# Moving the top-k pieces of two token tiles between pairs of gathered expert rows

## The reference

```python
v1, i1 = lax.top_k(s1, PEER_TOPK)
v2, i2 = lax.top_k(s2, PEER_TOPK)
cand = v1[..., :, None] + v2[..., None, :]          # 16 x 16 sums
top_s, top_c = lax.top_k(cand, PEER_TOPK)
...
act = gelu(einsum('ckd,cd->ck', expert_u[idx], x))
out = einsum('ck,ckd->cd', softmax(top_s) * act, expert_v[idx])
```

## Time and profile before

| | us |
|---|---|
| median of 3 runs | 3334.22 (3332.88 to 3334.69) |
| profiled execution | 3336.84 |
| its span | 3334.7 |
| TensorE, VectorE busy | 2621.3, 2133.8 |
| ScalarE, GpSimd busy | 1085.6, 1192.0 |
| first gather issued | 297.2 |
| moved by DMA | 1272.02 MB |

### The profile page before, as it was taken

One profiled execution on the slowest core, in us unless ns is written; L12 is line 12 of the kernel. 1 busy time (PEld: TensorE's weight loads), 2 busy tenths in 40 slices (PEclk: granted clock), 3 DMA queues, 4 the chain that ended last, 5 costly groups with the idle time before them and its releaser, 6 DMA issues.

```text
span 3334.7 us, 40436 instructions
## 1 busy us (share of the span) xinstructions
PE 2621.3 (79%) x14560; PEld 1321.0 (40%) x14560; DVE 2133.8 (64%) x4998; ACT 1085.6 (33%) x3411; POOL 1192.0 (36%) x1048
## 2 busy tenths in 40 slices
PE   8998878998888788998878777998885555555565
PEld 6775534564454344553444333554351111111111
DVE  2324669776568887775458878675448656765444
ACT  2112344332332643322323553332322232222222
POOL 0001333333334443333333443333334444444443
PEclk9999999999999899999899989999888777777777
DMA  4356999999999999999999989999999999999998
GB/s 135 112 158 242 416 385 343 399 392 402 404 416 417 409 398 417 418 417 415 415 417 408 396 349 413 418 418 416 412 415 405 412 420 421 419 417 412 420 421 337
DMA packets 224534, 1272.02 MB, mean 381 GB/s; under 512 B 24912, under 2 KB 26960, under 8 KB 93264
## 3 DMA queue, kind: packets, MB, share of 16 engines
q0 software_dynamic: 147456, 1073.81, 78.5%
q1 hardware_dynamic: 64128, 161.56, 13.2%
q10 hardware_dynamic: 12752, 34.08, 2.6%
HBM read 1256.78 MB, written 12.58 MB: 381 GB/s over the span
## 4 chain that ended last, share of the span: by engine, by line
DMA 39%; PE 34%; DVE 12%; issue 6%; ACT 5%; POOL 3%; ACTq 0%; POOLq 0%; DVEq 0%; SPq 0%
DMA rowsb<-uv,e_idx 38%; PE yacc L886 14%; PE mixp L583 7%; DVE rowsb L1678 5%; POOL rowsb L955 3%; PE mixp L608 3%; PE mixp L634 2%; PE mixp L595 2%; ACT diag L1241 2%; DVE area L1331 2%; ACT wg L1236 2%; PE mixp L645 2%; PE yacc L583 1%; DMA wt<-w_query_ 1%; ACT gmt L1222 1%
## 5 line engine op out<-in xcount | busy, mean ns | idle before, releaser
L955 POOL DMA_INDIRECT rowsb<-uv,e_idx x1024 | 1187.8, 1160 | 2114.9 <-PE yacc L886 1659.7
L1678 DVE CUSTOM_DVE_ANT_0 rowsb<-rowsb,hnrow 128x1024 f32<-128x1024 f32 x1024 | 1241.2, 1223 | 826.3 <-DMA rowsb<-uv,e_idx 824.5
L886 PE MATMUL yacc<-rowsb,diag 64*64 64x512 f32 x8192 | 1223.7, 722 | 660.7 <-ACT diag L1241 651.7
L886 PEld LDWEIGHTS yacc<-rowsb,diag 64*64 64x64 f32 x8192 | 300.0, 151 | 1406.7 <-ACT diag L1241 981.6
L1222 ACT ACTIVATE gmt<-dots 128x2 f32<-128x2 f32 x512 | 104.1, 203 | 1714.3 <-DVE dots L1678 1713.8
L583 PE MATMUL mixp<-area,wt 128*128 128x256 f32 x2144 | 497.7, 386 | 1.2 <-ACT area L1019 1.2
L583 PEld LDWEIGHTS mixp<-area,wt 128*128 128x128 f32 x2144 | 400.5, 191 | 128.3 <-issue 78.1
L1241 ACT ACTIVATE diag<-ident,wg 128x64 f32<-128x64 f32 x1024 | 300.3, 340 | 16.7
L1236 ACT ACTIVATE wg<-gmt,gate 128x1 f32<-128x1 f32 x1024 | 245.6, 286 | 17.7
L973 ACT ACTIVATE area<-mixp 128x512 f32<-128x512 f32 (+3 forms) x334 | 148.0, 487 | 290.6 <-PE mixp L583 167.7
L608 PE MATMUL mixp<-area,wt 128*128 128x256 f32 x960 | 229.2, 393 | 6.7 <-DMA wt<-w_query_ 6.7
(11 more groups left out here) (213 smaller groups left out, 1770.7 us busy)
## 6 DMA issues: line engine op xcount, KB each, us to landing
wt<-w_merge SPq DMA_DIRECT2D x96, 512.0 KB, 8.0
wt<-w_feat SPq DMA_DIRECT2D x80, 512.0 KB, 7.9
wt<-w_query_ SPq DMA_DIRECT2D x64, 512.0 KB, 12.1
wt<-w_tok SPq DMA_DIRECT2D x32, 512.0 KB, 10.7
wt<-w_out_ SPq DMA_DIRECT2D x32, 512.0 KB, 7.9
rowsb<-uv,e_idx POOLq DMA_INDIRECT x1024, 13.6
area<-x_rows ACTq DMA_DIRECT2D x4, 1024.0 KB, 12.4
area<-keysT ACTq DMA_DIRECT2D x16, 256.0 KB, 11.6
```

The costliest lines, as they stand in the source:

```text
L886: last = pe.matmul(yacc[at:at + HP, k % 2, c * NCH:(c + 1) * NCH], diag[r * HP:(r + 1) * HP, s, :], rowsb[r * HP:(r + 1) * HP, s, D + c * ...
L955: pool.indirect_dma_start(rowsb[:, n % RS, :], None, uv, bass.IndirectOffsetOnAxis(ap=e_idx[:, i % 2, k:k + 1], axis=0)).then_inc(row_load ...
L1678: dve.tensor_tensor_reduce(rowsb[:, s, 0:D], rowsb[:, s, 0:D], hnrow[:, i % HR, :], 1.0, 0.0, ALU.mult, ALU.add, dots[:, s:s + 1]).then_in ...
```

## The change

The table of the first 63 pieces becomes one piece in each of the pairs 2 to 37 and 57 to 83, numbered through the tiles, and none in 38 to 56. Before, there was one in each of 2 to 19, then 9 over pairs 20 to 39, then 36 over 40 to 82. The third group of the first tile's pieces listed here (heads 6 and 7) so ends at pair 28 in place of 39, and the second tile's four groups at 37, 65, 74 and 83 in place of 50, 61, 72 and 82. The load of the last scores and the softmax entries are moved with them, and the first tile's norm, final norm and store come three pairs later. The planner reads the table, so the steps of the second block may be laid otherwise.

```diff
--- before.py
+++ after.py
@@ -391,9 +391,9 @@
         cost = [load_of(b) for b in range(NB)]
         del cost[0][N_NORM + N_PROJ1:N_NORM + N_PROJ1 + n_sba(0)]
         TOP_EACH, BLOCK_END = 9, 36
-        SCORES_AT = (12, 13, 21, 41)
-        GATES = ((1, 0, 1, 1), (11, 0, 2, 2), (20, 0, 4, 2), (40, 0, 6, 2),
-                 (62, 1, 0, 2), (65, 1, 2, 2), (74, 1, 4, 2), (84, 1, 6, 2))
+        SCORES_AT = (12, 13, 21, 30)
+        GATES = ((1, 0, 1, 1), (11, 0, 2, 2), (20, 0, 4, 2), (30, 0, 6, 2),
+                 (62, 1, 0, 2), (67, 1, 2, 2), (76, 1, 4, 2), (85, 1, 6, 2))
         GATES_AT = {slot: n for n, (slot, i, first, count) in enumerate(GATES)}
         N_SLOT = TT * PP
         N_PARTS = 4 * TOP_EACH
@@ -407,14 +407,8 @@
                 else:
                     due = (p - 15) * N_PARTS // 42
                 parts_at[i][p] = max(0, min(due, N_PARTS)) - sum(parts_at[i][:p])
-        for n in range(83):
-            i, p = divmod(n, PP)
-            if n < 20:
-                parts_at[i][p] = 1 if n >= 2 else 0
-            elif n < 40:
-                parts_at[i][p] = (n - 19) * TOP_EACH // 20 - (n - 20) * TOP_EACH // 20
-            else:
-                parts_at[i][p] = (n - 39) * N_PARTS // 43 - (n - 40) * N_PARTS // 43
+        for n in [*range(2, 38), *range(57, 84)]:
+            parts_at[n // PP][n % PP] = 1
 
 
         def slot_load(s):
@@ -1261,11 +1255,11 @@
                     for p in range(PP):
                         gelu(i, p)
                         spread(i, p)
-                        if i == 1 and p == 19:
+                        if i == 1 and p == 22:
                             act.wait_ge(experts_ready, 8)
-                        if i > 0 and p == (19 if i == 1 else 3):
+                        if i > 0 and p == (22 if i == 1 else 3):
                             norm(i - 1)
-                        if i > 0 and p == (23 if i == 1 else 7):
+                        if i > 0 and p == (26 if i == 1 else 7):
                             store_out(i - 1)
                         if p == (36 if i == 1 else 20):
                             load_h(i)
@@ -1720,7 +1714,7 @@
                             next(parts, None)
                         if i * PP + p - 1 in GATES_AT:
                             gates(*GATES[GATES_AT[i * PP + p - 1]][1:])
-                        if i > 0 and p == (21 if i == 1 else 5):
+                        if i > 0 and p == (24 if i == 1 else 5):
                             final_norm(i - 1)
                         for b in range(NB):
                             for _n in range(steps[i * PP + p][b]):
```

## The result

The changed kernel takes 3347.18 us (median of 6 runs, 3342.95 to 3352.26) against 3333.55 (median of 6, 3330.93 to 3334.76) for the kernel before: a ratio of 1.0044, 95% interval 1.0033 to 1.0055, that is 11 to 18 us slower. The forecast was 3342.2, range 3331 to 3349. Its profiled execution took 3345.53 us with a span of 3343.3.

What follows compares the result with a forecast made beforehand. The expert stage was taken to be bound by bytes, VectorE and TensorE starving the transfers in places. Terms 7.8 + 0 + 3 + 0 - 2.8 = +8.0 us on the median 3334.22 gave 3342.2 us, range 3331 to 3349.

Steps and rivals of the forecast that it cites:

- What bounds the kernel: Expert stage, about 297 us to the end: bound by bytes; reordering can win only 35.6 us of transfers below their rate.
- Part 1: Pairs 24 to 37: added pieces less moved steps and a shorter wait make +5.3 us, 7.8 us more lost in transfers.
- Part 2: Quiet pairs 38 to 56: TensorE is full, so removing VectorE's pieces there gives nothing back, 0 us.
- Part 3: Pairs 57 to 83, 27 pieces for 22: crowding in pairs 62 to 66 costs 3 us, bounds 0 and 5.5.
- Part 4: Moved gate exponentials, score load, norm and store: nothing waits for them, 0 us.
- Part 5: Pairs 62 to 66: eight row buffers hide part of TensorE's lateness, 2.8 us off, bounds 0 and 6.
- C: Pairs 38 to 61: VectorE's pieces starve transfers, so the quiet pairs pay; -7 us, 3327; chance 0.15.
- B: Buffers hide the second half: part 3 nothing, part 5 its full size; +2 to +5 us, 3337; chance 0.25.
- D: Whole kernel: the change does not bind, planner's shift and pieces cancel; 3334; chance 0.10.

Runs made afterwards that it cites:

- e10_front_only: The kernel before with its steps and dates, but one piece in each of pairs 2 to 37 and the last 27 evenly over 38 to 82: ratio 1.0037.
- e2_pieces_only: The changed kernel with pieces and all dates as in the change, but the second block's steps laid as before: 3351.58 us, ratio 1.0057.
- e6_back_only: The kernel before, with 10 pieces evenly in pairs 38 to 56, 27 in 57 to 83 and the late dates, steps unmoved: ratio 1.0008.
- e1_shift_only: The kernel before with its pieces and dates, only the second block's steps laid as the changed planner lays them: 3337.38 us, ratio 1.0010.
- e4_dates_only: The kernel before with pieces and steps unmoved, only the second tile's gates and first tile's norm and store late: 3333.91 us, ratio 1.0006.

## Why the prediction was right, and where it was off

The forecast had the direction and most of the mechanism, but not the split, and that the measured time lies inside the range is partly luck. In the unit of its own sum, transfers below their rate: part 1 was 7.8 and measured 4.8, part 2 was 0 and measured 0.8 + 4.0, parts 3 and 5 together were 0.2 and measured 4.0, and 0.3 came behind. A first term too large by 3.0 covered a third of what the others lacked.

**What bounds the kernel**: right. The time is that of the transfers, and the sum of their losses gives the difference of the medians (14.0 against 13.6).

**Part 1, pairs 24 to 37**: the stretch was to take 96.1 + 5.3 and took 101.3 us, where the working gives 101.4. Pair 38 itself came at 573.8 for 575.7, since pair 24 started 1.7 us earlier. The price of a piece read from pairs with and without one held, with unmoved steps too: 12.7 us for 12.5 worked out (`e10_front_only`). Where the softmax and the score load moved to pair 30 with the pieces it was 19.3 (`e2_pieces_only`). Its loss in transfers came out smaller, 4.8 for 7.8, because 325 GB/s were still moved. (The heading's "eight more" is a slip, the text's 8 and 18 are right; it enters no sum.)

**Part 2, the quiet pairs**: that they give nothing back was right. VectorE has 72.85 us of work in place of 94.81 between these sums, and the stretch is still 138.4 us long, where 136.6 were worked out; with 12 or 17 pieces in it it is no longer (136.8, 137.9). The Trainium skill, Perfetto Trace Analysis, section Identifying the Most-Contended Engine, holds matmul busy time to be no good measure and judges TensorE's headroom by the weight-load share among others. Here that share was 56%, and it was no room: this case goes with the busy time. The size was off. In transfers, 0 was forecast and 4.8 us were lost more, with 385 GB/s in place of 398: filling pair 52 was counted as 1.9 us less of TensorE and not as transfers that find less time. The sum of pair 42 came at 604.15 for 602.4, that of pair 62 at 742.51 for 739.0, so +9.95 for +6.4. Part of it is in pairs 38 to 42: 26.5 us, where 6.2 and three times 5.60 were taken. These rows of the changed kernel's TensorE show it:

```profile
569.65 3.69 PE L880 MATMUL yacc<-rowsb,diag 64*64 64x512 f32 x16 [5.56 <-ACT diag L1235]
573.27 4.72 PE L577 MATMUL mixp<-area,wt 128*128 128x256 f32 x16
577.92 0.60 PE L732 MATMUL mixp<-ident,area 4*128 4x4 f32 x4
578.45 1.95 PE L880 MATMUL yacc<-rowsb,diag 64*64 64x512 f32 x16
580.33 3.72 PE L577 MATMUL mixp<-area,wt 128*128 128x256 f32 x16
585.77 1.95 PE L880 MATMUL yacc<-rowsb,diag 64*64 64x512 f32 x16 [1.73 <-ACT diag L1235]
```

It had stood still for 5.56 us while VectorE was behind; the sum and the weight unit that follow take 3.69 and 4.72 us for 1.95 and 3.72, VectorE waits 2.36 us for the small matmul behind them (L732), and then each waits for the other once more (1.73). Two engines that each need 5.6 and 5.5 us a pair took 6.6 here, not the larger of the two.

**Part 3, the crowd**: mechanism and place were right (pair 64, the residual, TensorE's wait for it), the size was not: from the sum of pair 62 to that of pair 66 (774.69) it took 32.2 us, before 24.8 (757.34), +7.4 for the 3 that I took and the 5.5 of the upper bound. (By the prices of part 1 the five pieces are 10.1 us and not 10.3.) I had the normalizer's steps beside the residual in the text, but counted only the pieces; the reciprocal in the same pair and the lower clock of TensorE's sum and unit were left out. Between the same two sums the crowd alone adds 3.4 us (28.2, `e6_back_only` and `e2_pieces_only`) and the shift alone 1.8 (26.6, `e1_shift_only`). So the 3 fits the crowd by itself; the shift's 1.8 and 2.2 more where the two meet were not counted.

**Part 4, dates**: the late ones are right, 0 (`e4_dates_only`, 1.0006, interval across 1, at most 5 us). For the softmax at pair 30, 0 fits the change, where VectorE has no wait for it, but the reason given is not enough. That its scores are ready does not make it free: it puts two table loads of 1.28 us in front of a gelu, and with unmoved steps pair 38 came 6.6 us later for it. That the planner had emptied just pair 30 was luck. No run moves this date alone.

**Part 5, what the buffers hide**: right in kind, too small. At TensorE's sums the forecast was 6.4 + 1.25 (the weight unit not yet fetched) + 3 - 2.8 = 7.9; measured it is 9.95 + 1.25 + 7.4 = 18.6 by pair 66, of which 13.6 arrived, so 5.0 were hidden. (The 1.25 stayed an estimate. Without it the traces say 17.35 us at the sum of pair 66 and 12.1 at pair 100, 5.2 hidden.) The terms that failed are those of pairs 38 to 61 (short by 3.6) and 62 to 66 (short by 4.4); 2.2 of these 8 us the larger cover took back.

**The rivals**: C, that the quiet pairs pay, fell with TensorE's stretch, which is as long with 17 pieces as with 5. B is out by its size, and by the 4.0 us lost around pairs 62 to 66. D is out. The planner's shift, which the prediction worked out, was as written, pair for pair.

**The signs**: pair 38 (573.8 for 576), TensorE still full (134.4 of 138.4 us) and a stretch above 136 us came as said. Pairs 24 to 37 moved 325 GB/s, where below 325 was said. The GB/s in TensorE's stretch did not stay as before (385 for 398). The distance was not constant from 780 us on: 10.7 us at pair 80, 12.1 at pair 100. The last sign of being wrong, a distance at pair 100 that differs much from that at pair 66, is met by TensorE's sums (17.4 at pair 66) and not by the starts on VectorE (13.1): the buffers hid more than was taken off.

## What to carry to other kernels

Where several engines share a stage almost level, a gap in one engine's work pays only if that engine is the last one there; ask for each moved piece which wait it now fills and which it now precedes, and ask the same of every small entry that moves with it, on its own engine. Price a stage in the unit of what bounds the whole (here the time the transfers run below their rate), once, and check it against the late engine's own times, where a wait between two engines shows that the other account hides. And let a planner's answer be part of the prediction: with unmoved steps the same pieces and dates cost 19 us, with the moved ones 14 to 15, though the intervals overlap. When two variants differ at the end, look first for the pair at which their traces part.

## What the hardware showed that I had not expected

TensorE after 5.56 and 4.95 us without work: the next sum took 3.69 us where most take 1.95, and the weight unit behind it 4.72 and 4.43 for 3.72; the granted clock of the stretch from 742.5 to 785 us was 0.92 on the mean, against 1.00 in the kernel that has this gap closed. So a wait of some 5 us cost TensorE 2.5 to 2.7 us more behind it. The kernel before pays this too: 3.69 us after 5.29 without work (the sum at 805.4 us), and 3.39 after 2.57 (at 574.2), while after 2.90 and 2.40 (at 552.6 and 613.1) a sum took 1.95. Whether that time reached the end was not tried by itself.
